# One table-set load in front of the attention's heads instead of two in every head

## What is computed

```
sc = einsum('bhqd,bhkd->bhqk', qb, kb) * scale          # softmax attention (MLA)
w  = softmax(where(mask, sc, -inf));   o_mla = w @ v

z      = einsum('bhqd,bhkd->bhqk', qb, kb) * scale      # stick-breaking attention
log_1m = where(mask, log_sigmoid(-z), 0.0)
suffix = cumsum(log_1m, reverse=True) - log_1m
a      = where(mask, exp(log_sigmoid(z) + suffix), 0.0);   o_sb = a @ sv
```

## Time and profile before

| | us |
|---|---|
| median of 3 runs | 2465.91 |
| lowest and highest run | 2461.06, 2466.99 |
| the profiled execution | 2461.6 |
| its span | 2460.3 |
| PE busy | 2351.5 (96%) |
| ACT busy | 457.7 (19%) |
| DVE busy | 1084.0 (44%) |
| POOL busy | 1337.5 (54%) |

### The profile page before, as it was taken

How to read it: one execution, slowest core, us unless ns; L and a number is a source line. 1 busy time by engine, 2 the same in 40 slices (tenths; PEclk the granted TensorE clock), 3 DMA queues, 4 the chain that set the end, 5 groups by cost and what they waited for, 6 DMA issues and landing times.

```text
span 2460.3 us, 25206 instructions
## 1 busy us (share of the span) xinstructions
PE 2351.5 (96%) x10496; PEld 1898.6 (77%) x10496; DVE 1084.0 (44%) x1116; ACT 457.7 (19%) x633; POOL 1337.5 (54%) x706
## 2 busy tenths in 40 slices
PE   7999998898898999998999999999889999999998
PEld 6888886687766888886888887878656787888887
DVE  3344213677456444302443433332557774434335
ACT  3111002222312111101111100111268421111001
POOL 4666665654016666665666665556200265666664
PEclk9999999999679999999999999999989999999999
DMA  4323321221002233321233322223100132333322
GB/s 160 96 94 102 113 85 54 79 73 61 9 15 63 94 96 102 108 95 54 94 94 102 112 98 81 82 86 104 36 9 1 36 95 84 97 100 107 112 92 67
DMA packets 51977, 199.44 MB, mean 81 GB/s; under 512 B 6008, under 2 KB 6136, under 8 KB 51736
## 3 DMA queue, kind: packets, MB, share of 16 engines
q1 hardware_dynamic: 48816, 191.52, 24.6%
q10 hardware_dynamic: 3048, 6.31, 0.7%
HBM read 195.70 MB, written 2.10 MB: 80 GB/s over the span
## 4 chain that ended last, share of the span: by engine, by line
PE 66%; DVE 4%; ACT 3%; issue 1%; POOL 1%; DMA 0%; DVEq 0%; ACTq 0%
PE psum L286 20%; PE psum L287 19%; PE psum L288 19%; PE psum L334 1%; PE psum L752 1%; DVE scratch L1845 1%; PE psum L744 1%; PE psum L386 1%; PE psum L498 1%; POOL x L267 1%; ACT work L1179 1%; DVE work L1754 0%; PE psum L568 0%; DVE scratch L1255 0%; ACT L1179 0%
## 5 line engine op out<-in xcount | busy, mean ns | idle before, releaser
L257 POOL TENSOR_SCALAR w_hi<-w_raw 128x1024 fp32r<-128x1024 f32 (+3 forms) x339 | 388.5, 1146 | 1036.7 <-PE psum L288 884.5
L259 POOL TENSOR_TENSOR w_lo<-w_raw,w_hi 128x1024 fp32r<-128x1024 f32 (+3 forms) x339 | 915.1, 2699 | 28.2
L286 PE MATMUL psum<-u_hi,w_hi 128*128 128x512 f32 x2104 | 843.2, 401 | 34.6 <-DVE u_lo L1296 25.2
L287 PE MATMUL psum<-u_hi,w_lo 128*128 128x512 f32 x2104 | 824.7, 392 | 0.0
L288 PE MATMUL psum<-u_lo,w_hi 128*128 128x512 f32 x2104 | 824.4, 392 | 0.0
L286 PEld LDWEIGHTS psum<-u_hi,w_hi 128*128 128x128 f32 x2104 | 398.7, 189 | 133.9 <-issue 39.8
L287 PEld LDWEIGHTS psum<-u_hi,w_lo 128*128 128x128 f32 x2104 | 398.3, 189 | 90.5 <-issue 9.9
L288 PEld LDWEIGHTS psum<-u_lo,w_hi 128*128 128x128 f32 x2104 | 398.0, 189 | 83.1
L288 PE MATMUL psum<-hidden_lo,w_hi 128*128 128x512 f32 (+1 forms) x824 | 321.7, 390 | 0.0
L286 PE MATMUL psum<-hidden_hi,w_hi 128*128 128x512 f32 x784 | 305.9, 390 | 1.1 <-DVE hidden_lo L1848 1.1
L287 PE MATMUL psum<-hidden_hi,w_lo 128*128 128x512 f32 x784 | 305.4, 390 | 0.0
(11 more groups left out here) (255 smaller groups left out, 1647.2 us busy)
## 6 DMA issues: line engine op xcount, KB each, us to landing
w_raw<-in_ffn_in SPq DMA_DIRECT2D x176, 512.0 KB, 3.5
w_raw<-in_ffn_out SPq DMA_DIRECT2D x64, 704.0 KB, 4.1
w_raw<-in_proj_in SPq DMA_DIRECT2D x34, 512.0 KB, 3.5
w_raw<-in_mix_in SPq DMA_DIRECT2D x29, 512.0 KB, 3.5
w_raw<-in_embed SPq DMA_DIRECT2D x8, 640.0 KB, 4.0
w_raw<-in_mix_out SPq DMA_DIRECT2D x8, 512.0 KB, 3.5
w_raw<-in_branch SPq DMA_DIRECT2D x8, 512.0 KB, 3.6
w_raw<-in_proj_out SPq DMA_DIRECT2D x8, 512.0 KB, 3.6
```

What stands on the lines that cost most here:

```text
L257: pool.tensor_scalar(hi, raw, 1.0, 1.0, ALU.mult, ALU.mult).then_inc(k.w_split, 1)
L259: pool.tensor_tensor(lo, raw, hi.bitcast(F32), ALU.subtract).then_inc(k.w_split, 1)
L286: pe.matmul(out, hi[:, cols], xhi, start=first, stop=False)
L287: pe.matmul(out, lo[:, cols], xhi, start=False, stop=False)
```

## The change

One line is added in `act_attend`, between the definitions and the loop over the heads:

```
--- before.py
+++ after.py
@@ -1191,6 +1191,7 @@
             act.wait_ge(k.z_out, h + 1)
             act.copy(tile(k.uhi, n), H.o[n]).then_inc(k.pair_hi, 1)
 
+    act.preload_act_table_set("natural_log_exp_and_others")
     for h in range(AH):
         s = H.soft[h % 2]
         stick_logits(h)
```

## The result

| | before | changed |
|---|---|---|
| median of 5 runs | 2461.24 us | 2449.78 us |
| lowest and highest | 2460.92, 2466.99 | 2449.62, 2453.10 |
| the profiled execution, its span | 2461.6, 2460.3 | 2449.78, 2448.5 |
| PE busy | 2351.5 | 2345.6 |
| ACT busy | 457.7 | 437.0 |

The quotient of the two medians themselves is 0.9953, 11.5 us. The forecast was 2454.8 us. The time lies in the range given, but the change is nearly twice the 6.4 us that the forecast time implies against this median.

The account below looks back on a forecast made before the run. PE was taken to idle 0.97 us in six steps waiting for ACT, whose table loads lie on the chain. 6.2 (waits) + 0.3 (step 7) + 4.6 (clock falls) = 11.1 us off 2465.9 gave 2454.8 us, range 2447 to 2461.

Parts of the forecast that it names:

- What is paid is PE's wait, not the load: Steps 1 to 6: L744 starts 1.04 us earlier, not 2.59; six waits give 6.2 us.
- Step 0 and the added load: nothing: Added load hidden behind the norms' square root; step 0's three removed loads gain nothing, its exponents awaiting the negated maxima.
- Step 7 and the tail: 0.3 us: After the last L744, the cast L1205 moves by about 0.3 us until the mask ends; what follows moves as a block.
- The falls: 4.6 us: PE stretches from L744 to the sums' end: without waits, three clock falls of 1.54 us go, 4.6 us.
- The sum: 6.2 + 0.3 + 4.6 = 11.1 us; the profiled execution would go from 2461.6 to 2450.5 us.
- I take the sum off the median: The 11.1 us subtracted from the median of three runs, 2465.9 us, giving 2454.8 us.
- Another wait in place: Rival: PE waits 0.6 us at the stick sums in each of six steps, falls stay; 2463 us, chance 0.08.
- the spare times of 0.2 and 0.4 us at the two halves of the sums: Predicted slack before PE's stick sums: 0.4 us for the high part (first half), 0.2 us for the low part (second).
- All loads in full: Rival: 2.59 us of load comes off each of steps 1 to 7; with falls 22.7 us, 2443 us, chance 0.05.
- Slower sets: Rival of no gain: the new set's exponential or logarithm takes longer than 1.27 us on ACT; 2466 us, chance 0.03.
- More falls: Rival: PE's unbroken small groups from L744 on get 1.2 GHz more often, 1.54 us per fall; 2474 us, chance 0.03.

Follow-up runs that it names:

- e1_one_load: Changed kernel with one load of the same set put back between logarithm and exponents in steps 1 to 7; 2450.32 us, ratio 0.9954 to the kernel before.
- e3_filled_wait: Kernel before, all loads in place, with two spare matmuls on PE ahead of L744 in steps 2 to 7; 2459.29 us, ratio 0.9990.
- e4_idle_no_loads: Changed kernel with L744 of steps 2 to 7 also waiting for the rounding of the previous head's softplus; 2472.21 us.
- r2_before: Third profile of the kernel before, unchanged; 2460.97 us.
- r1_before: Second profile of the kernel before, unchanged; 2460.47 us.
- r3_after: Changed kernel profiled once more, unchanged; profiled execution 2464.88 us, ratio to the kernel before 0.9968.
- e5_ends: Changed kernel with two loads of the same set put back around the logarithm in steps 0 and 7 only; 2450.71 us in one run.
- r4_before: A further profile of the kernel before, unchanged, which caught a higher level; 2474.22 us.
- e2_two_loads: Changed kernel with two loads of the same set put back in steps 1 to 7, one each side of the logarithm; 2464.79 us, ratio 1.0015.

## Why the prediction was right in its mechanism and wrong in its size

- **What is paid is PE's wait, not the load.** Right. 1.04 us a step and 13.66 us a step were predicted; 1847.83 - 1834.17 = 13.66. e1_one_load shows the 1.3 us of spare time directly.
- **Step 0 and the added load: nothing.** Right; the added load ran from 1797.29, with 2.01 us of idleness left behind it.
- **Step 7 and the tail: 0.3 us.** PE's last wait went from 2.21 us to 1.95, so 0.26 us. Right. That what follows moves as a block is not quite so: see the sum.
- **The falls: 4.6 us.** Right, and by the cause given: e3_filled_wait takes 4.65 us less with them gone and the steps as long as before, and e4_idle_no_loads brings them without loads. That it was three of six was read from one execution; r2_before has a single fall of 2.8 us, and against it the stage gains 9.3 us.
- **The sum.** 11.1 us for the stage; measured 108.73 - 97.57 = 11.16 us between the profiles. The rest of the profiled difference of 11.8 us lies outside: 0.7 us lost ahead of step 0, 1.7 us won between L744 of step 0 and of step 1 (3.63 against 4.63 us in L744 alone), 0.4 us lost behind the stage. The 1.7 us are not the change's: r1_before, with all the loads, takes 23.64 us there as the changed kernel does (23.63), and e1_one_load, r3_after and e5_ends take 25.1 to 25.3. The 0.4 us are there against r1_before too, and what they come from was not followed.
- **The step that failed: "I take the sum off the median".** The term that was mis-sized is the time to start from, 2465.9 us, which five runs put at 2461.24. The sum itself gave 2450.5 us from the profiled execution, 0.7 us from the median measured. The three runs shown had two high ones, 2465.91 and 2466.99, and their median lay 4.7 us above the one of five runs, 2461.24. The prediction saw that the runs differed by four falls' worth and still treated the median as the kernel's time. In r4_before and r3_after the higher level comes from the clock ahead of the heads; no trace of the two high runs exists, so for them the place is not shown. A difference worked out from rows belongs to the execution that the rows are of. The forecast thereby implied 6.4 us against the median of five runs, where 11.5 us were measured and 11.1 us worked out. That those two agree so well is in part luck: the later medians are 8.0 us apart.
- **The rivals.** Another wait in place: none showed; the spare times of 0.2 and 0.4 us at the two halves of the sums held. All loads in full: refuted by e1_one_load. Slower sets: Exp and Ln take 1.27 and 1.26 us from the new set. More falls: none in the heads in any profile without the wait.

## What to carry to other kernels

A load of 1.28 us on the chain of work is worth only what the engine at the end of the chain is idle for. Read that engine's idle time per turn, and what stands behind the next engine, before adding up loads. Idleness of about a us per turn on TensorE may cost more than itself: here six waits of 0.97 us had 4.6 us of falls of the clock on top, and filling them with spare matmuls removed the falls in the one profile taken of it. And put a difference worked out from a trace against the time of that trace's execution, not against the median of a few runs, when the runs of one kernel differ by several us.

## What the runs showed of the hardware that was not expected

- A load of the set that is already in takes as long as a switch, 1.28 us (e1_one_load, e2_two_loads), and is executed each time it is written.
- One kernel on one core has executions up to 17.5 us apart (2460.13 to 2477.66 us in 23 runs). In the two pairs of profiles that show a lower and a higher level, the time lies where the granted clock is lower, ahead of the heads (0.64 against 0.69 in the mixer); from the end of the heads to the end of the program the clock is 0.99 on both.
- Spare matmuls of 64 rows and 256 columns, 1.13 us for each pair, went with a granted clock of 1.00, the 2.4 GHz level, in six steps of one profile, where in four of five profiles of the kernel before and of e2_two_loads it fell in three.
